# Row transfers of a mixture of experts moved from SyncE's queue to GpSimd's, with the first rows turned late and a gate folded in quarters

## The reference

```python
def moe_swiglu(h, router, w_gate, w_up, w_down):
    ht = h.reshape(bsz * seq, d)
    probs = jax.nn.softmax((ht @ router).astype(jnp.float32), axis=-1)
    vals, idx = lax.top_k(probs, TOP_K)
    wts = vals / jnp.sum(vals, axis=-1, keepdims=True)
    gates = jnp.einsum('tk,tke->te', wts, jax.nn.one_hot(idx, N_EXPERTS, dtype=jnp.float32)).astype(h.dtype)
    out = jnp.zeros_like(ht)
    for e in range(N_EXPERTS):
        out = out + gates[:, e:e + 1] * swiglu(ht, w_gate[e], w_up[e], w_down[e])
```

## Time and profile before

| what | us |
|---|---|
| median of three runs (1313.1 to 1315.42) | 1314.25 |
| the profiled execution, its own time | 1318.11 |
| its span, first to last instruction | 1316.0 |
| TensorE busy | 1271.8 |
| VectorE busy | 928.2 |
| ScalarE busy | 821.0 |
| mean granted clock of TensorE | 0.997 |

### The profile page before, as it was taken

One profiled execution on the slowest core, in us unless ns is written; L12 is line 12 of the kernel. 1 busy time (PEld: TensorE's weight loads), 2 busy tenths in 40 slices (PEclk: granted clock), 3 DMA queues, 4 the chain that ended last, 5 costly groups with the idle time before them and its releaser, 6 DMA issues.

```text
span 1316.0 us, 15842 instructions
## 1 busy us (share of the span) xinstructions
PE 1271.8 (97%) x6057; PEld 1035.7 (79%) x6057; DVE 928.2 (71%) x926; ACT 821.0 (62%) x905; POOL 40.8 (3%) x52
## 2 busy tenths in 40 slices
PE   8999999999999899999999999999999998999998
PEld 6888888788887788877887788767778886788886
DVE  4685455446768978898889988898877573655542
ACT  5646444336866777798778878877577665544431
POOL 4001000000000200000000000002010000000000
PEclk9999999999999999999999999999999999999999
DMA  9648655553327999999999999999683241555540
GB/s 321 231 140 270 214 180 190 170 156 122 112 97 303 354 423 400 370 386 421 397 401 392 422 405 380 404 353 397 240 288 128 97 160 64 195 189 192 170 150 32
DMA packets 89855, 339.45 MB, mean 258 GB/s; under 512 B 6267, under 2 KB 14160, under 8 KB 66128
## 3 DMA queue, kind: packets, MB, share of 16 engines
q1 hardware_dynamic: 86816, 328.64, 66.8%
q0 software_dynamic: 2816, 9.89, 2.2%
q10 hardware_dynamic: 160, 0.07, 0.0%
HBM read 332.02 MB, written 9.44 MB: 259 GB/s over the span
## 4 chain that ended last, share of the span: by engine, by line
PE 77%; DVE 11%; issue 6%; ACT 3%; DMA 2%; POOL 0%; DVEq 0%; ACTq 0%
PE bank L1905 23%; PE bank L1907 23%; PE bank L1906 23%; DVE w_lo L390 7%; PE bank L2268 1%; DMA moe_slots_in<-h,row_to 1%; PE bank L2017 1%; PE bank L2277 1%; ACT w_hi L385 1%; PE bank L2000 1%; PE bank L2278 1%; PE bank L2044 1%; PE bank L2260 1%; POOL moe_slots_in L610 0%; DVE x L1197 0%
## 5 line engine op out<-in xcount | busy, mean ns | idle before, releaser
L390 DVE TENSOR_TENSOR w_lo<-raw,w_hi 128x2048 fp32r<-128x2048 f32 (+3 forms) x218 | 484.7, 2239 | 196.6 <-ACT w_hi L385 195.9
L385 ACT ACTIVATE w_hi<-raw 128x2048 fp32r<-128x2048 f32 (+3 forms) x218 | 407.2, 1877 | 212.5 <-PE bank L1907 202.6
L1905 PE MATMUL bank<-w_hi,xT_hi 128*128 128x512 f32 (+2 forms) x672 | 257.2, 383 | 3.6 <-DVE xT_lo L1169 1.7
L1907 PE MATMUL bank<-w_hi,xT_lo 128*128 128x512 f32 (+2 forms) x672 | 253.9, 378 | 0.0
L1906 PE MATMUL bank<-w_lo,xT_hi 128*128 128x512 f32 (+2 forms) x672 | 253.8, 378 | 0.0
L1905 PEld LDWEIGHTS bank<-w_hi,xT_hi 128*128 128x128 f32 x672 | 127.3, 189 | 27.7 <-issue 3.5
L1907 PEld LDWEIGHTS bank<-w_hi,xT_lo 128*128 128x128 f32 x672 | 127.1, 189 | 23.1
L1906 PEld LDWEIGHTS bank<-w_lo,xT_hi 128*128 128x128 f32 x672 | 127.4, 190 | 22.0
L1905 PE MATMUL bank<-w_hi,gT_hi 128*128 128x512 f32 x320 | 127.7, 399 | 2.1 <-DVE w_lo L390 1.7
L1907 PE MATMUL bank<-w_hi,gT_lo 128*128 128x512 f32 x320 | 126.6, 396 | 0.0
L1906 PE MATMUL bank<-w_lo,gT_hi 128*128 128x512 f32 x320 | 126.5, 395 | 0.0
(11 more groups left out here) (428 smaller groups left out, 1748.2 us busy)
## 6 DMA issues: line engine op xcount, KB each, us to landing
raw<-in_moe_w_gate SPq DMA_DIRECT2D x34, 1024.0 KB, 8.1
raw<-in_moe_w_up SPq DMA_DIRECT2D x34, 1024.0 KB, 7.9
raw<-in_moe_w_down SPq DMA_DIRECT2D x32, 1024.0 KB, 12.1
raw<-in_w_gate_up SPq DMA_DIRECT2D x22, 1024.0 KB, 5.1
raw_beside<-in_moe_w_down SPq DMA_DIRECT2D x18, 1024.0 KB, 12.2
raw_beside<-in_moe_w_gate SPq DMA_DIRECT2D x16, 1024.0 KB, 6.8
raw_beside<-in_moe_w_up SPq DMA_DIRECT2D x16, 1024.0 KB, 7.8
back<-in_moe_w_gate SPq DMA_DIRECT2D x14, 1024.0 KB, 7.5
```

Source lines behind the costliest of these rows:

```text
L385: nc.scalar.activation(w_hi[:, slot, :n], raw_of(i, stream, ring)[:, :n], ACT.Copy).then_inc(stream.high, 1)
L390: nc.vector.tensor_tensor(w_lo[:, slot, :n], raw_of(i, stream, ring)[:, :n], w_hi[:, slot, :n].bitcast(F32), ALU.subtract).then_inc(stream ...
L1905: mm(dst, a_hi, b_hi, start=start, stop=False)
L1907: return mm(dst, a_lo, b_hi, start=False, stop=stop)
```

## The change

- The stores of results and the loads of rows leave SyncE's stream. GpSimd issues them in one row: store of zeros, then the wait for the scatters, then for each position a load (`read_rows`) and a store. They wait only for their data and for the buffer, not for a chunk's turn.
- In expert 0 (`late_rows`, on VectorE `first`) the rows are transposed ahead of the seventh of the eight down chunks and not ahead of the first; the numbers of the jobs follow, and ScalarE and VectorE copy the rows in step 21 and not in 15 and 16.
- In a light expert the gate is folded by quarters behind up's third to sixth chunk; up's last two chunks run one after the other; the rows are transposed ahead of the fold of up and not behind it; ScalarE copies up a step later (15), and VectorE splits chunk 18 ahead of the first product and not behind it.
- `REGION_PAD` is 16 and not 24.

```diff
-REGION_PAD = 24
+REGION_PAD = 16
...
 SyncE:
-                        if c == 13:
-                            store_rows(p)
-                        if c == (14 if p else 20) and p < E - 1:
-                            load_rows(p + 1)
...
 GpSimd:
+                def store_rows(p):
+                    at_, n = (FIRST_SLOT[p - 1] + P, SLOTS_AT[p - 1]) if p else (0, P)
+                    pool.wait_ge(sem("moe_y"), 1 + p)
+                    pool.dma_start(slots_out[at_:at_ + n, :], M["y"][:n, :]).then_inc(sem("moe_rows_stored"), 16)
+
+                def read_rows(p):
+                    at_, n = FIRST_SLOT[p], SLOTS_AT[p]
+                    pool.wait_ge(sem("moe_job"), first_job(p - 1))
+                    pool.dma_start(M["rows_in"][:n, :], slots_in[at_:at_ + n, :]).then_inc(sem("moe_rows_loaded"), 16)
...
+                store_rows(0)
+                pool.wait_ge(sem("moe_dispatched"), 16 * 2 * T)
+                for p in range(1, E):
+                    read_rows(p)
+                    store_rows(p)
...
 ScalarE, light:
                         if c == 14:
                             light_silu(i)
+                        if c == 15:
                             for quarter in range(QUARTERS):
                                 light_up(e, i, quarter)
...
 ScalarE, expert:
                         if c == 15:
                             turn_high(number + 1, 1)
-                            rows_high(number + 2, 0, 0)
+                            if not late_rows:
+                                rows_high(number + 2, 0, 0)
                         if c == 16:
-                            rows_high(number + 3, 1, 1)
-                            turn_high(number + 4, 2)
+                            if not late_rows:
+                                rows_high(number + 3, 1, 1)
+                            turn_high(number + (2 if late_rows else 4), 2)
                         if c == 17:
-                            turn_high(number + 5, 3)
+                            turn_high(number + (3 if late_rows else 5), 3)
+                        if c == 21 and late_rows:
+                            rows_high(number + 4, 0, 0)
+                            rows_high(number + 5, 1, 1)
...
 VectorE, light (in expert() the same edits as on ScalarE, with first):
                     for c in range(EXPERT_CHUNKS):
+                        split_low(MOE0 + c + AHEAD, e, W1)
                         if c == 15:
                             light_product(e, i, 0)
                             light_low(e, 0)
-                        split_low(MOE0 + c + AHEAD, e, W1)
-                        if c == 15:
                             light_product(e, i, 1)
...
 TensorE:
+                def next_rows(e):
+                    pe.wait_ge(sem("moe_rows_loaded"), 16 + 16 * e)
+                    turn_rows(bank[0], 0)
+                    turn_rows(bank[1], 1)
...
-                    for k in range(KD - 2):
+                    for k in range(KD):
                         wh, wl = weights(W1, MOE0 + KD + k, e)
                         for quarter in range(QUARTERS):
                             ins = light_product(4 + quarter, k, wh, wl, quarter)
+                            if k == KD - 1 and quarter < QUARTERS - 1:
+                                ins.then_inc(sem("light_in_psum"), 1)
                         ins.then_inc(W1.used, 1)
...
+                        if k == 2:
+                            pe.wait_ge(sem("light_copied"), gate_copied(i))
+                        if 2 <= k < 2 + QUARTERS:
+                            ins = fold_quarter(M["e_act"], 2 + (k - 2) // 2, k - 2)
+                            if k == 1 + QUARTERS:
+                                ins.then_inc(sem("light_in_psum"), 1)
+                    next_rows(e)
                     pe.wait_ge(sem("moe_silu_done"), gated(e, 1))
...
                     up(e, h, 2)
                     turn_act(e, 1, 2)
-                    pe.wait_ge(sem("moe_rows_loaded"), 16 + 16 * e)
-                    turn_rows(bank[0], 0)
-                    turn_rows(bank[1], 1)
+                    if not late_rows:
+                        next_rows(e)
                     for c in range(FE // 256):
                         if c in (0, 2, 4, 6):
-                            pe.wait_ge(sem("moe_drained"), number + (1, 2, 5, 6)[c // 2])
+                            pe.wait_ge(sem("moe_drained"), number + ((1, 2, 3, 4) if late_rows else (1, 2, 5, 6))[c // 2])
+                        if c == 6 and late_rows:
+                            next_rows(e)
```

More of the change, by code:

```diff
@@ L506, in _ @@
             if "moe" in parts:
[L507 to L520, removed]
                 for p in range(E):
@@ L612, in _, with first_job @@
                             M["h"][:, t, :], None).then_inc(sem("moe_dispatched"), 16)
+                def store_rows(p):
[6 more added lines that the diff above has]
+                    pool.dma_start(M["rows_in"][:n, :], slots_in[at_:at_ + n, :]).then_inc(sem("moe_rows_loaded"), 16)
+                def first_job(p):
+                    i = (p - 1) // 2
+                    return (heavy_of_pair(i)[2] if p % 2 else light_of_pair(i)[1]) if p else GATHER_JOBS
+                store_rows(0)
[3 more added lines that the diff above has]
+                    store_rows(p)
                 pool.wait_ge(sem("moe_rows_stored"), 16 * E)
@@ L959, in light, with expert @@
                     ins.then_inc(sem("light_copied"), 1)
-                def expert(e, number, rows_high):
+                def expert(e, number, rows_high, late_rows=False):
                     for c in range(EXPERT_CHUNKS):
@@ L1007, in _ @@
                     ins.then_inc(sem("moe_job_high"), 1)
-                expert(0, GATHER_JOBS, rows_high)
+                expert(0, GATHER_JOBS, rows_high, late_rows=True)
                 with act.Fori(0, PAIRS) as i:
@@ L1642, in expert @@
                             turn_low(n_high + 1, 1)
-                            rows_low(n_high + 2, 0, 0)
+                            if not first:
+                                rows_low(n_high + 2, 0, 0)
                         if c == 16:
-                            rows_low(n_high + 3, 1, 1)
-                            turn_low(n_high + 4, 2)
+                            if not first:
+                                rows_low(n_high + 3, 1, 1)
+                            turn_low(n_high + (2 if first else 4), 2)
                         if c == 17:
-                            turn_low(n_high + 5, 3)
+                            turn_low(n_high + (3 if first else 5), 3)
+                        if c == 21 and first:
+                            rows_low(n_high + 4, 0, 0)
+                            rows_low(n_high + 5, 1, 1)
                 def take_back(choice, t):
@@ L2317, in light @@
                             ins = light_product(4 + quarter, k, wh, wl, quarter)
+                            if k == KD - 1 and quarter < QUARTERS - 1:
+                                ins.then_inc(sem("light_in_psum"), 1)
                         ins.then_inc(W1.used, 1)
[L2319 to L2322, removed]
-                    last_two = [(k, weights(W1, MOE0 + KD + k, e)) for k in (KD - 2, KD - 1)]
-                    for quarter in range(QUARTERS):
-                        for k, (wh, wl) in last_two:
-                            ins = light_product(4 + quarter, k, wh, wl, quarter)
-                            if quarter == QUARTERS - 1:
-                                ins.then_inc(W1.used, 1)
-                        if quarter < QUARTERS - 1:
-                            ins.then_inc(sem("light_in_psum"), 1)
+                        if k == 2:
[5 more added lines that the diff above has]
+                    next_rows(e)
                     pe.wait_ge(sem("moe_silu_done"), gated(e, 1))
@@ L2365, in first_expert, with rest_of_expert @@
                         ins.then_inc(W1.used, 1)
-                    rest_of_expert(0, 0, GATHER_JOBS)
-                def rest_of_expert(e, h, number):
+                    rest_of_expert(0, 0, GATHER_JOBS, late_rows=True)
+                def rest_of_expert(e, h, number, late_rows=False):
                     pe.wait_ge(sem("moe_y"), 1 + e)
```

3 lines of the change are left out of this document (removed).

## The result

The changed kernel takes 1296.76 us (median of 4 runs, 1294.6 to 1297.55), the one before 1314.84 in the same comparison (4 runs, 1313.1 to 1316.45): a ratio of 0.986, 95% interval 0.9842 to 0.9879, or 15.9 to 20.8 us gained. Forecast were 1303.4 and a range that ended at 1299.6.

What follows compares the result with a forecast made beforehand. TensorE, busy 97% of the span, was taken as the bound, so only idle or slowed time could be won: 4.5 + 5.1 + 1.3 = 10.9 us, giving 1303.4 us. Range 1299.6 to 1307.8, or to 1309.2 with Rival A and Rival B.

Steps and rivals of the forecast that it cites:

- Eight words less pad: Buffers in the region: shifting them changes nothing, since VectorE's splits take 2285 ns inside and outside; 0, within 0.5 us.
- First rows late: Expert 0: later transposes remove TensorE's 2.80 us wait and 1.7 us of low clock; 4.5 us gained, bounds 3.5 and 4.7.
- Rival B: Expert 0: expert 1's rows late at the seventh down chunk, through GpSimd's issue or the zeros; gain 6.2, 1308.0; chance 0.08.
- Light experts: Three light experts: gate folded in quarters behind chunks removes part of the waiting; 1.7 us each, 5.1 us in all.
- Rival A: Light experts: weights bind, so the new order gains nothing there; total gain 5.8, 1308.5; chance 0.10.
- Last expert: Last expert: earlier gathers remove TensorE's 1.26 us wait for a late weight chunk; 1.3 gained, bounds 3.2 gained and 2 lost.
- Zeros ahead of the rows: Expert 0, GpSimd's queue: zeros and rows, 1 MB more, take 7.5 us; rows land at 465 to 467, leaving 8 us.
- The rule weighed against the change: GpSimd's queue: VectorE's two-port instructions delay its descriptors, each transfer some 2.5 us later; covered by slack, sum unchanged.

Runs made afterwards that it cites:

- e4: Kernel before with only expert 1's rows transposed six down chunks later, all transfers still on SyncE: 1312.34 us, ratio 0.9977.
- e2: Changed kernel with REGION_PAD back at 24 words, so all of the change except the pad: 1307.2 us, ratio 0.9936.
- e5: Kernel before with only the light experts' new order of folds, transposes and splits: 1309.93 us, ratio 0.9961.
- e9: Changed kernel with the last expert's gathers held until eleven of its weight chunks are split, where they began before: 1295.75 us, ratio 0.9854.
- e14: Changed kernel with stores and loads of expert rows back on SyncE's queue: 1296.83 us, ratio 0.9859.
- e3: Kernel before with only the row transfers moved to GpSimd's queue, which also starts the last gathers early: 1320.72 us, ratio 1.0045.
- e10: Changed kernel with 32 bytes added ahead of w_hi and none taken back, shifting moving and stationary operands alike: 1298.29 us, ratio 0.9861.
- e12: Kernel before with row transfers on GpSimd's queue, but expert 1's rows loaded ahead of the store of zeros: 1319.85 us, ratio 1.0046.
- e1: Kernel before with only REGION_PAD cut from 24 to 16 words: 1306.69 us, ratio 0.994.

## Why the prediction was wrong

The step that failed is the last of the sum: "Eight words less pad shift what lies in the region: splits from a buffer inside it and from one outside take 2285 ns each, so 0, within 0.5 us over all." It measured 6.1 to 9.7 us alone and, beside late rows, 10.4 by the medians (1307.2 to 1296.76) or 11.4 by the spans (1304.2 to 1292.8). The earlier trace rows are right and answer for VectorE alone. The region also holds TensorE's stationary operands, and TensorE is the engine that leads. Its rows for the same question could be had from the trace of before, 391 ns with xT and 396 with gT; the page itself has 396 for gT, but for xT a mean of three shapes, 378, so the groups have to be asked for by shape. What the pad sets isn't an alignment of one buffer but the distance from w_hi and w_lo: 32 bytes off a multiple of 256 before, none after.

The other steps, point by point:

- **First rows late, 4.5 us (3.5 to 4.7).** The trace gives 4.56 us in e4 and 4.57 in e2; the medians of e4 only 2.0 to 4.2. The profiled execution of before was 3.3 to 3.9 us above the medians; the forecast moved its sum over to the median whole, as if every execution had this wait and this low clock. By the mean clocks (e4) the 1.7 us of low clock are what most executions lack; that is estimated, not shown. Landing at 465 to 467 was forecast, 461.6 it was, against a need at 470.3 (475 forecast): 8.7 us to spare where 8 were. Rival B did not come.
- **Light experts, 1.7 each (5.1).** 1.40 each in the trace of e5, 4.2 in all; 5.1 by its ratio (3.3 to 6.8). The forecast's walk holds: VectorE's wait of 2.73 us is 0.30. Rival A did not come: with the change no chunk of weights was late in that stage.
- **Last expert, 1.3 (-2 to 3.2).** Too small for the medians (e9, e14). In the traces the stage took 83.70 us before, 82.85 in e3 and 82.23 in e2, so 0.9 to 1.5 us less. The old late chunk is gone and a new one stands in its place, which the prediction had only in its bounds. This stage also differs between executions of one order, 81.62 us in the changed kernel and 82.98 in e10.
- **Zeros ahead of the rows.** Zeros and rows together were priced as 7.5 us from the last scatter to the rows' landing, covered by slack. It was 9.8 us from the issue of the rows' load, and slack did cover it in the whole change. Alone the move costs 4.1 to 7.8 us (e3), but the zeros are not the cause (e12). What the queue is worth in the whole change is below what the runs can tell (e14).

Without the pad the kernel was 6.6 to 10.3 us faster (e2), and 1307.2 us lies inside the range of 1299.6 to 1309.2. The sum of 10.9 us is above that interval, so the priced terms were a little too high, while the one put at nothing was worth about 10; the two errors have opposite signs and the second is four times the first. The rule weighed against the change, by the Trainium skill (SBUF — State Buffer, "SBUF: two separate sides"), was to slow GpSimd's descriptors beside VectorE. It shows, in a place where it cost nothing; the changed kernel's GpSimd in the last expert:

```profile
867.28 6.48 POOL L618 DMA_INDIRECT back<-moe_slots_out,row_from  x1 [6.88 <-DMA moe_slots_out<-y]
874.06 6.60 POOL L618 DMA_INDIRECT back<-moe_slots_out,row_from  x1 [0.30 <-issue]
880.97 2.11 POOL L618 DMA_INDIRECT back<-moe_slots_out,row_from  x1 [0.31 <-issue]
883.38 2.62 POOL L618 DMA_INDIRECT back<-moe_slots_out,row_from  x1 [0.30 <-issue]
```

The first two took 6.5 us where VectorE was busy 13.27 of 13.40 us. In e9 all four took 2.2 to 2.6 where it was busy 8.89 of 10.60. The trace agrees with the rule in direction, and the size is of the same order: 4.1 us more for each gather, where the two figures of the Trainium skill, 0.62 and 3.1 us, are 2.5 apart. It isn't VectorE's busy share alone: the third gather of e9 took 2.46 us with VectorE busy for 2.29 of them.

## What to carry to other kernels

- A shift of addresses is priced on every engine that reads the moved buffers, the leading one first. Compare the mean of one instruction form between operands inside and outside what moves: 391 against 396 ns was in the trace of before, and 5 ns times 2,736 is not small.
- For matmuls of this form (fp32r, 128x128 stationary, 512 columns moving) place the stationary and moving operands so that they start a multiple of 256 bytes apart in the partition, and look at the pitch again whenever a buffer ahead of them changes size.
- Try the parts of a bundle apart. Here one was a loss alone (queue, +5.5 us) and no loss in company, and one line of eight words carried about half of the gain.
- A stall read from one profiled execution is that execution's. If it lies 3.9 us above the median, ask whether the stall is what makes the difference before its whole price goes into the sum.

## What the runs showed of the hardware

- The pitch (the distance between two starts) of 128x512 fp32r matmuls depends on the distance between the start addresses of the stationary and the moving operand: 227 ns at 0 and 256 bytes, 233.2 to 233.4 at 32, 64 and 224, 232.8 at 128 (modulo 256). Distances between those were not tried. The weight load's own duration did not follow it (188 ns with gT before and after), so what collides and where stays open. The Trainium skill (TensorE: Matmul & The Clock Gate, "Step-by-step: what each phase is for") has TensorE read the two operands through two independent ports, so that loading the next weights takes nothing from the running matmul. By that the pad would be worth nothing; these runs differ by 6.3 ns for each matmul, and the measurement decides.
- This was measured with 512 columns. Other widths go otherwise. With xT at distance 0 the 128x256 matmuls stood 119.8 ns apart (w_hi with xT_lo), at 32 bytes 118.4: the other sign, and small. The 128x352 ones went from 159.5 to 161.4, and cT's with 384 columns stayed at 173 with either pad (before and after).
- A wait of TensorE cost clock too, and not in proportion to its length: over the 15 us from 455 on the granted clock was 0.89 with the wait of 2.80 us (before) and 0.77 with those of 3.27, 4.09, 6.09 and 8.05 (e5, e1, e12, e3), so 1.7 us of work lost and 3.4.
- A load of 512 KB landed 3.3 us after its issue with no weights issued beside it (before, e4), and 8.0 to 9.8 us amid weights (e3, e12, the changed kernel).
